# Layer norm's steps among other units, low parts and small parameters behind the sums that units wait for, splits for the keys ahead of those for the queries

## The chip, the core and the metric

One core of a Trainium2 chip runs the kernel. The metric is the time of one execution on the device, in microseconds (us); shorter is better. Five engines work side by side, each in the order of its own program, and are held together by semaphores: TensorE (PE in the profile, PEld for its weight loads), VectorE (DVE), ScalarE (ACT), GpSimd (POOL) and SyncE (SP), which here starts the transfers.

## The reference, cut to what matters

A block of 512 tokens by 1024 features passes through four layers in float32. The parts that the change touches:

```
# even mixer (first layer)
u  = causal_conv(a_val * sigmoid(a_glu), 31 taps)
ya = silu(layernorm(u, ln_g, ln_b)) * silu(a_gate)     # mean, then variance of u - mean
yb = pool branch * silu(b_gate)
h  = h + concat(ya, yb) @ w_out
# odd mixer (second layer): starts with rmsnorm(h, norm_odd) @ w_in
# third layer, at its end
gate = sigmoid(rmsnorm(h, norm_ple) @ w_ple_gate)      # 8 units "gate0"
h    = h + gate * (p @ w_ple_proj)
hk   = rmsnorm(h, kv_norm);   k = rope(hk @ w_k);  v = hk @ w_v
hn   = rmsnorm(h, norm_mix);  q = rope(hn @ w_q)       # fourth layer, attention
```

The third layer's mixer (a state space model) needs some small parameters (powers of a complex number per state) that depend on the inputs alone.

## The kernel before, in words

Everything is held transposed: features on the 128 partitions, the 512 tokens along the free dimension, so `h` is 8 chunks `H[:, c, :]` of 128x512. The weights come in 281 **units** of 128x1024 (8 blocks of 128x128), in the order of the list `ORDER`. A product in float32 precision is made of three faster ones: each operand x is split into a high part (rounded to fp32r) and a low part (what is left), and hi*hi + hi*lo + lo*hi is summed in one PSUM bank. A unit is thus 24 matmuls of 128x512 on TensorE.

For weight unit i, `high` (line 276, ScalarE) makes `WH` once SyncE has fetched `RAW` and unit i-3 is done (3 buffers); `low` (line 280, GpSimd) makes `WL`; SyncE fetches into `RAW` again behind it. The loops of ScalarE and GpSimd call `highs(n + 4)` and `lows(n + 4)` in step n, so the work for unit n+3 is queued there, and everything written behind it in that step waits for unit n. `linear` (line 291) issues one unit: 16 matmuls first, then the 8 with the low weights; with `ready` it waits, chunk by chunk, for the high parts of the input (`x_hi`, ScalarE, line 413), then for the low ones (`x_lo`, VectorE, line 417 or 421), and it wants `WL` from its start.

**Even mixer.** `EVEN` lists the steps: K0 to K7 are the 8 units of `yb @ w_out`, O0 to O7 those of `ya @ w_out`. The convolution's taps (VectorE, line 587) are spread over the steps up to K1. GpSimd adds the 8 chunks into `LS` (`conv_sums`, line 724); TensorE makes the mean behind K2 (line 487); VectorE subtracts it (line 663), ScalarE squares (line 348), GpSimd and VectorE add the squares (lines 357, 363); TensorE sums them over the partitions behind K4 (`stat_sums`, line 375); VectorE adds eps (line 381), GpSimd takes the root (line 386), TensorE spreads it over the partitions inside K5 (`stat_spread`, line 394). In step K6 VectorE and ScalarE then work on each chunk in turn: times the root (line 674), silu (ScalarE, line 563), times the gate (line 682), high and low part of `ya`. O0 waits for these chunks. In steps O0 to O7 VectorE adds each unit's result to `H` (`add_to_h`, line 428), ScalarE makes the high part and a square of it, VectorE the low part for the odd mixer (line 421) and ten of the small parameters' instructions (`dve_params`, lines 1113 to 1184, 128x32 each, in a chain). X0 is the odd mixer's first unit.

**Gates of the third layer.** `pe_ple` runs the 8 units gate0. Per chunk c: VectorE scales the unit's result (`scaled`, line 410), ScalarE takes the sigmoid (line 1950), VectorE multiplies by `PJ` (line 1966) and adds to `H` (line 1969), ScalarE makes two high parts (for keys `P2h`, for queries `P0h`) and a square, VectorE two low parts, GpSimd adds the square. ScalarE does the sigmoid of chunk n and the three operations of chunk n-2 in step n, behind `highs`. The units wk (keys) wait for `P2h` and `P2l` chunk by chunk.

Of the kernel before, what the change touches and what calls it, by code (L numbers as in the profile page):

```python
# [71 lines left out]
TAPS = 6  # L72
PX_AT = {1: 0, 2: 1, 4: 2, 5: 3}
# [66 lines left out]
def program(nc, ctx, known, D):  # L140
# [150 lines left out]
    def linear(pe, what, xh, xl, chunks, freed_by, ready=None, half=None, first=False):  # L291
# [14 lines left out]
        for n, c in enumerate(chunks):  # L306
# [12 lines left out]
            if half and n == 5:  # L319
                half()  # L320
# [129 lines left out]
    def pe_even(pe):  # L450
# [4 lines left out]
        for n, (kind, c) in enumerate(EVEN):  # L455
            what = even_what(n)
            if kind in "GABFS":
                linear(pe, what, P0h, P0l, range(8), "evac_d", "even" if n == 0 else None,
                       {2: lambda: stat_sums(pe, "even", True), 3: lambda: spread_even(pe)}.get(n), n == 0)
# [23 lines left out]
            if (kind, c) == ("K", 2):  # L483
                b, before = banks.take("mean", "ln_sub")
                pe.wait_ge(*at(*before))
                pe.wait_ge(*at("conv_sum", 7))
                pe.matmul(b[:, :], MEAN[:, :], LS[:, :], start=True, stop=True).then_inc(*inc("ln_mean", 0))
            elif (kind, c) == ("K", 4):
                stat_sums(pe, "ln", True)
# [6 lines left out]
    def act_even(act):  # L496
# [37 lines left out]
    def act_even_follow(act, n, s):  # L534
# [18 lines left out]
        elif kind == "K" and s == 0 and c == 2:  # L553
            for i in range(8):
                act.wait_ge(*at("ln_sub", i if i < 7 else "mean"))
                square(act, "ln", i, chunk(i), True)
        elif kind == "K" and s == 0 and c == 6:
            for i in range(9):
                if i < 8:
                    act.wait_ge(*at("ln_n", i if i < 7 else ("spread", "ln")))  # L560
                    if i > 1:
                        act.wait_ge(*at("x_lo", ("ya", i - 2)))
                    act.activation(CB[i % 2][:, :], chunk(i), ACT.Silu, bias=vec("ln_a_b", i),
                                   scale=vec("ln_a_g", i)).then_inc(*inc("ln_silu", i))
                if i > 0:
                    act.wait_ge(*at("ln_y", i - 1))
                    split_hi(act, "ya", i - 1, E2h[:, i - 1, :], CB[(i - 1) % 2][:, :])
                if i == 4:
                    highs(act, IDX[what] + 5)
        elif kind == "O" and s == 0:  # L570
            norm_in_act(act, "odd", c, [("odd", P0h, vec("norm_odd", c))], what)
            if c < 4:
                act_params(act, c)
# [49 lines left out]
    def dve_even_follow(dve, n, s, parameters):  # L623
# [34 lines left out]
        elif kind == "K" and s == 0:  # L658
            if c == 3:
# [8 lines left out]
            elif c == 5:  # L668
                stat_mean(dve, "ln", 1e-5)
            elif c == 6:  # L670
# [30 lines left out]
    def pool_even(pool):  # L701
# [8 lines left out]
        for n in range(len(EVEN) + 3):  # L710
            for s in (3, 2, 1, 0):
                if s == 0 and n < len(EVEN):
                    lows(pool, n + 4)
# [13 lines left out]
    def pool_even_follow(pool, n, s):  # L727
# [32 lines left out]
        elif kind == "K" and s == 0 and c == 2:  # L760
            conv_sums(pool, 3)
            for i in range(8):
                add_square(pool, "ln", i, True)
            stat_root(pool, "ln")
# [1165 lines left out]
    def ple_outs(l, n):  # L1930
        if l:
            return []
        return [("kv", P2h, vec("kv_norm", n)), ("att", P0h, vec("norm_mix", 8 + n))]

    def act_ple(act, l):
        for n in range(9):
            if n < 8:
                highs(act, IDX[(f"gate{l}", 0, n)] + 4)
                if n == 1:
                    stat_copy(act, f"ple{l}")  # L1940
                    act_ple_gate(act, l, 0)
                if n > 0:
                    act_ple_gate(act, l, n)
            if n > 1:
                norm_in_act(act, "out" if l else "att", n - 2, ple_outs(l, n - 2), ("ple", l, n - 2), l == 1)
        norm_in_act(act, "out" if l else "att", 7, ple_outs(l, 7), ("ple", l, 7), l == 1)
# [5 lines left out]
    def dve_ple(dve, l):  # L1952
        for n in range(10):
            if n == 0:
                stat_mean(dve, f"ple{l}")
                continue
            if n == 1:
                scaled(dve, tmp(2), (f"gate{l}", 0, 0), f"ple{l}").then_inc(*inc("evac_d", (f"gate{l}", 0, 0)))
            if n < 8:
                scaled(dve, tmp(2 + n % 4), (f"gate{l}", 0, n), f"ple{l}").then_inc(*inc("evac_d", (f"gate{l}", 0, n)))  # L1960
            if n < 9:
                c = n - 1
                s = tmp(2 + c % 4)
                dve.wait_ge(*at("ple_sig", (l, c)))
                dve.wait_ge(*at("evac_a", ("pj", l, c)))
                dve.tensor_tensor(s, s, PJ[:, c, :], ALU.mult).then_inc(*inc("ple_y", (l, c)))
                dve.wait_ge(*at("ple_y", (l, c)))
                dve.wait_ge(*at("h", (f"down{l}", 3, c)))
# [599 lines left out]
```

## Time and profile before

| | us |
|---|---|
| median of 3 runs | 1908.15 |
| lowest and highest of them | 1906.16, 1908.15 |
| the profiled execution | 1902.84 |
| its span in the trace | 1901.02 |
| TensorE busy | 1776.7 (93% of the span) |
| GpSimd, VectorE, ScalarE busy | 976.5, 894.8, 760.5 |

The profile page and the trace are of one execution. In a timeline a row gives the start and the duration of one or several like instructions, and in square brackets how long the engine had been idle before it and what released it. Matmuls overlap in a timeline: their pace is the distance of their starts. The granted clock is TensorE's, as a share of 2.4 GHz; its two levels are 2.4 and 1.2 GHz.

### The profile page before, as it was taken

Reading aid. Unit: us, or ns where it says so; the run is one execution under the profiler, and the core shown is the slowest. Engines: PE = TensorE matmul, PEld = TensorE weight load, DVE = VectorE, ACT = ScalarE, POOL = GpSimd, SP = SyncE. Lnnn points to the kernel's source line nnn. Section 1 sums busy time; section 2 is a strip of 40 time slices with the busy share of each in tenths; the row PEclk is TensorE's granted clock in tenths of the full one; section 3 lists DMA queues with packets and bytes.
Section 4 is the critical chain, followed back from the end, with each engine's and each line's share of the span. In section 5 each row is a group of like instructions: output and inputs, shape, how many; then the busy total and the mean of one; then the engine's idle time right before and its main releaser. Section 6 shows DMA issues by size and latency. Waiting matters only on the chain.

```text
span 1901.0 us, 20872 instructions
## 1 busy us (share of the span) xinstructions
PE 1776.7 (93%) x7994; PEld 1440.6 (76%) x7994; DVE 894.8 (47%) x1297; ACT 760.5 (40%) x1194; POOL 976.5 (51%) x613
## 2 busy tenths in 40 slices
PE   9999988999998889999999999897888999999996
PEld 7887876777777777888888888674456888888885
DVE  3999956676665874622121213723452221212125
ACT  5233324377765553343232323422454432323242
POOL 5869544577555564644444445652234544444462
PEclk9999999999998899999999999897889999999998
DMA  4323213222221233222232222220001222232221
GB/s 160 109 78 111 100 67 102 87 79 89 89 80 48 80 104 106 94 100 93 95 100 100 90 98 97 70 87 25 23 22 46 99 96 93 100 100 93 96 100 45
DMA packets 55107, 164.04 MB, mean 86 GB/s; under 512 B 6368, under 2 KB 14176, under 8 KB 54880
## 3 DMA queue, kind: packets, MB, share of 16 engines
q1 hardware_dynamic: 55008, 162.71, 25.4%
q8 instruction: 64, 1.05, 0.2%
q14 instruction: 35, 0.29, 0.0%
HBM read 156.66 MB, written 6.03 MB: 86 GB/s over the span
## 4 chain that ended last, share of the span: by engine, by line
PE 67%; DVE 11%; issue 8%; ACT 7%; POOL 7%; DMA 0%; SPq 0%; POOLq 0%; DVEq 0%; ACTq 0%
PE B L304 57%; DVE B L587 3%; POOL WL L280 3%; PE B L287 1%; ACT WH L276 1%; PE B L289 1%; PE B L288 1%; PE B L1616 1%; PE B L2162 1%; PE B L1509 1%; PE B L2144 1%; DVE P0l L421 1%; DVE SW L1113 1%; POOL TMP L2127 1%; ACT TMP L2112 1%
## 5 line engine op out<-in xcount | busy, mean ns | idle before, releaser
L280 POOL TENSOR_TENSOR WL<-RAW,WH 128x1024 fp32r<-128x1024 f32 x281 | 682.8, 2432 | 712.7 <-ACT WH L276 712.7
L276 ACT ACTIVATE WH<-RAW 128x1024 fp32r<-128x1024 f32 x281 | 296.8, 1059 | 743.6 <-PE B L304 713.0
L304 PE MATMUL B<-P0h,WH 128*128 128x512 f32 x1128 | 444.1, 394 | 5.9 <-ACT P0h L413 3.9
L304 PE MATMUL B<-P0l,WH 128*128 128x512 f32 x1128 | 437.0, 393 | 1.0 <-DVE P0l L421 1.0
L304 PE MATMUL B<-P0h,WL 128*128 128x512 f32 x1128 | 284.9, 390 | 2.3 <-POOL WL L280 2.3
L304 PEld LDWEIGHTS B<-P0h,WH 128*128 128x128 f32 x1128 | 213.0, 189 | 55.5 <-issue 5.6
L304 PEld LDWEIGHTS B<-P0l,WH 128*128 128x128 f32 x1128 | 213.8, 190 | 46.3 <-DVE P0l L421 1.5
L304 PEld LDWEIGHTS B<-P0h,WL 128*128 128x128 f32 x1128 | 211.9, 188 | 46.6 <-POOL WL L280 2.7
L428 DVE TENSOR_TENSOR H<-H,B 128x512 f32<-128x512 f32 x96 | 65.8, 686 | 318.9 <-PE B L304 318.9
L304 PE MATMUL B<-P1h,WH 128*128 128x512 f32 x512 | 199.7, 390 | 1.4 <-DVE P1l L417 1.4
L304 PE MATMUL B<-P1l,WH 128*128 128x512 f32 x512 | 194.7, 389 | 0.0
L1882 DVE SCALAR_TENSOR_TENSOR TMP<-B,RS 128x512 f32<-128x512 f32 x64 | 44.1, 691 | 258.4 <-PE B L304 244.0
L587 DVE SCALAR_TENSOR_TENSOR B<-UP,VE,B 128x512 f32<-128x512 f32 x232 | 156.5, 750 | 1.6 <-ACT B L531 1.6
L304 PE MATMUL B<-P1h,WL 128*128 128x512 f32 x512 | 131.0, 389 | 0.0
L304 PEld LDWEIGHTS B<-P1h,WH 128*128 128x128 f32 x512 | 96.1, 188 | 22.1 <-DVE P1l L417 2.3
L304 PEld LDWEIGHTS B<-P1h,WL 128*128 128x128 f32 x512 | 96.1, 188 | 19.9
L304 PEld LDWEIGHTS B<-P1l,WH 128*128 128x128 f32 x512 | 96.1, 188 | 19.9
L357 POOL TENSOR_TENSOR ACC<-ACC,TMP 128x512 f32<-128x512 f32 x51 | 74.1, 1453 | 52.7 <-ACT TMP L348 52.5
L304 PE MATMUL B<-P2h,WH 128*128 128x512 f32 x144 | 56.7, 394 | 9.0 <-ACT P2h L413 9.0
L304 PE MATMUL B<-P2l,WH 128*128 128x512 f32 x144 | 54.3, 402 | 0.0
L421 DVE SCALAR_TENSOR_TENSOR P0l<-H,VE,P0h 128x512 fp32r<-128x512 f32 x40 | 46.0, 1161 | 13.6 <-ACT P0h L413 13.6
L2127 POOL TENSOR_SCALAR TMP<-TMP,AS 128x256 f32<-128x256 f32 (+1 forms) x64 | 27.9, 456 | 44.6 <-DVE AS L2121 44.6
(327 smaller groups left out, 2676.5 us busy)
## 6 DMA issues: line engine op xcount, KB each, us to landing
RAW<-in_w SPq DMA_DIRECT2D x281, 512.0 KB, 3.2
H<-in_xT SPq DMA_DIRECT2D x8, 256.0 KB, 4.6
g<-GB SPq DMA_DIRECT2D x8, 256.0 KB, 2.1
GB<-g SPq DMA_DIRECT2D x32, 64.0 KB, 2.0
out<-TMP SPq DMA_DIRECT2D x8, 256.0 KB, 2.1
u<-TMP SPq DMA_DIRECT2D x7, 256.0 KB, 2.0
U<-u SPq DMA_DIRECT2D x28, 64.0 KB, 2.0
SPT<-in_ssm SPq DMA_DIRECT2D x1, 1040.0 KB, 5.7
```

What stands on the lines that cost most here:

```text
L276: act.activation(WH[:, i % NS, :], RAW[:, i % NR, :], ACT.Copy).then_inc(*inc("w_hi", i))
L280: pool.tensor_tensor(WL[:, i % NS, :], RAW[:, i % NR, :], WH[:, i % NS, :].bitcast(F32), ALU.subtract).then_inc(*inc("w_lo", i))
L287: pe.matmul(out, wh, xh, start=start, stop=False)
L288: pe.matmul(out, wl, xh, start=False, stop=False)
L289: return pe.matmul(out, wh, xl, start=False, stop=stop)
L304: return pe.matmul(b[:, :], w[:, ws[c]], x[:, c, :], start=start, stop=stop)
L357: pool.tensor_tensor(ACC[:, :], ACC[:, :], tmp(c % 2), ALU.add).then_inc(*inc("acc", (k, c)))
L421: dve.scalar_tensor_tensor(dst, src, g, hi.bitcast(F32), ALU.mult, ALU.subtract).then_inc(*inc("x_lo", (k, c)))
L428: dve.tensor_tensor(H[:, n, :], H[:, n, :], banks.bank[what][:, :], ALU.add).then_inc(*inc("h", key))
L587: dve.scalar_tensor_tensor(chunk(c) if j == 30 else CB[c % 2][:, :], UP[:, c, j:j + T], w, CB[c % 2][:, :], ALU.mult, ALU.add).then_inc(*i ...
L1882: dve.scalar_tensor_tensor(mlp_tmp(q, c), banks.bank[what][:, :], 0.0, rs(f"mlp{l}"), ALU.max, ALU.mult).then_inc(*inc("evac_d", what))
L2127: pool.tensor_scalar(s_head(n, h), s_head(n, h), st[:, 16 + h:17 + h], 1.0, ALU.mult, ALU.mult).then_inc(*inc("att_w", (n, h)))
```

## The change

The same instructions are issued, with other places in the engines' orders.

1. **Layer norm.** GpSimd sums the last two conv chunks in step K1, ahead of `low` for that step (it was K2, behind it). The mean's matmul stands inside unit K2, behind its fifth chunk. ScalarE's squares and GpSimd's sums of squares and root come in step K2 ahead of `highs` and `lows`. VectorE subtracts in step K2 (it was K3). The sums over the partitions and the spread are inside K4 (behind chunks 1 and 7), and VectorE and ScalarE do the chain for `ya` in step K4 (it was K6), with the high weights of three units in between.
2. **Small parameters.** 12 of their instructions behind `add_to_h` in each of steps O0 to O4 (it was 10 behind the low part in each of O1 to O6); ScalarE's first function of them moves to K7.
3. **Gates and queries.** ScalarE works on chunk n, and not n-2, behind the sigmoid of chunk n. VectorE makes the low part for the keys of chunk c-1 behind the scaling of chunk c, and the low parts for the queries later: three during the gates, five in `dve_att`. GpSimd adds chunk n's square in step n (it was n+1). The gates of the last layer stay as they are, in functions of their own.

```diff
             elif kind == "K":
                 linear(pe, what, E1h, E1l, range(8), "h", "yb" if c == 0 else None,
-                       (lambda: stat_spread(pe, "ln")) if c == 5 else None)
+                       {2: {4: lambda: ln_mean(pe)},
+                        4: {1: lambda: stat_sums(pe, "ln", True), 7: lambda: stat_spread(pe, "ln")}}.get(c, {}))
...
# ScalarE, in step n
                 if s == 0 and n < len(EVEN):
+                    if EVEN[n] == ("K", 2):
+                        act_ln_squares(act)
+                    elif EVEN[n] == ("K", 4):
+                        act_ln(act, n)
                     highs(act, n + 4)
...
+            if i in (1, 3, 6):
+                highs(act, n + 4 + (1, 3, 6).index(i))
...
# VectorE
         elif kind == "K" and s == 0:
-            if c == 3:
+            if c == 2:
                 dve.wait_ge(*at("ln_mean", 0))
...
-            elif c == 5:
+            elif c == 4:
                 stat_mean(dve, "ln", 1e-5)
-            elif c == 6:
                 dve.wait_ge(*at("stat_spread", "ln"))
...
         elif kind == "O" and s == 0:
             add_to_h(dve, what, c, what, what_k(c))
+            if c < 5:
+                for _ in range(PARAMETERS):
+                    next(parameters, None)
         elif kind == "O" and s == 1:
             split_lo_scaled(dve, "odd", c, P0l[:, c, :], H[:, c, :], vec("norm_odd", c), P0h[:, c, :])
-            if c < 6:
-                for _ in range(10):
-                    next(parameters, None)
...
# GpSimd, in step n
                 if s == 0 and n < len(EVEN):
+                    if EVEN[n] == ("K", 1):
+                        conv_sums(pool, 3)
+                    elif EVEN[n] == ("K", 2):
+                        for i in range(8):
+                            add_square(pool, "ln", i, True)
+                        stat_root(pool, "ln")
                     lows(pool, n + 4)
...
+    def act_ple(act):
+        for n in range(8):
+            highs(act, IDX[("gate0", 0, n)] + 4)
+            if n == 1:
+                stat_copy(act, "ple0")
+            for c in ([0, 1] if n == 1 else [n] if n else []):
+                act_ple_gate(act, 0, c)
+                norm_in_act(act, "att", c, ple_outs(c), ("ple", 0, c))
...
+    def dve_ple(dve):
+
+        stat_mean(dve, "ple0")
+        for c in range(8):
+            scaled(dve, tmp(2 + c % 4), ("gate0", 0, c), "ple0").then_inc(*inc("evac_d", ("gate0", 0, c)))
+            if c > 0:
+                dve_kv(dve, c - 1)
+            dve_ple_sum(dve, 0, c)
+            if c in (2, 3, 4):
+                dve_q_in(dve, [c - 2])
+        dve_kv(dve, 7)
...
     def pool_ple(pool, l):
...
-            if n > 0:
-                add_square(pool, "out" if l else "att", n - 1, l == 1)
+            if l == 0 and n < 8:
+                add_square(pool, "att", n)
+            elif l and n > 0:
+                add_square(pool, "out", n - 1, True)
...
     def dve_att(dve):
+        dve_q_in(dve, (3, 4))
         stat_mean(dve, "att")
+        dve_q_in(dve, (5, 6))
         dve.wait_ge(*at("stat_root", "att"))
         dve.tensor_copy(RK[:, :], SM[:, 8:12]).then_inc(*inc("v_root", 0))
+        dve_q_in(dve, [7])
         dve_rope_in(dve, ("k", 0))
```

## Rows read from the trace of the kernel before

**Rows 1.** Windows, from K2's end to O0's: stretch, length, busy time by engine, granted clock, DMA share, GB/s.
```profile
258.00:317.00 59.00, 45.45 (x187) 34.70 (x186) 26.80 (x43) 21.23 (x30) 23.81 (x13) 0.88 0.24 81
```
**Rows 2.** Timeline of TensorE, K2 to the start of O1: start, duration, what.
```profile
260.20 1.98 PE L304 MATMUL B<-E1h,WL 128*128 128x512 f32 x8
268.34 2.04 PE L487 MATMUL B<-LS,MEAN 128*128 128x512 f32 x2 [6.17 <-POOL LS L724]
...
316.75 0.39 PE L304 MATMUL B<-E2h,WH 128*128 128x512 f32 x1
```
**Rows 3.** Timeline of TensorE around X0: its start, its wait, what follows it.
```profile
354.83 0.39 PE L304 MATMUL B<-P0h,WH 128*128 128x512 f32 x1
...
360.73 0.79 PE L304 MATMUL B<-P0h,WH 128*128 128x512 f32 x1 [3.02 <-ACT P0h L413]
...
367.19 0.95 PE L375 MATMUL B<-MEAN,ACC 128*128 128x1 f32 x8
```
**Rows 4.** Timeline of TensorE: last gate, wait in wk0, what follows it.
```profile
1207.42 1.98 PE L304 MATMUL B<-P1h,WL 128*128 128x512 f32 x8
...
1222.11 0.80 PE L304 MATMUL B<-P2h,WH 128*128 128x512 f32 x1 [6.08 <-ACT P2h L413]
...
1226.55 1.26 PE L375 MATMUL B<-MEAN,ACC 128*128 128x1 f32 x8
```
**Rows 5.** Timeline of GpSimd: the low part of a weight, then the last two conv sums.
```profile
263.40 2.34 POOL L280 TENSOR_TENSOR WL<-RAW,WH 128x1024 fp32r<-128x1024 f32 x1 [3.04 <-ACT WH L276]
265.70 2.49 POOL L724 TENSOR_TENSOR LS<-LS,UP 128x512 f32<-128x512 f32 x2
```
**Rows 6.** Timeline of VectorE: last taps, subtraction of the mean, last sum of squares.
```profile
254.57 1.40 DVE L587 SCALAR_TENSOR_TENSOR UP<-UP,VE,B 128x512 f32<-128x512 f32 x2
...
270.42 3.68 DVE L663 TENSOR_TENSOR UP<-UP,B 128x512 f32<-128x512 f32 x6 [7.52 <-PE B L487]
...
277.75 1.35 DVE L363 TENSOR_TENSOR TMP<-TMP 128x512 f32<-128x512 f32 x1 [0.76 <-ACT TMP L348]
```
**Rows 7.** Chain in order of time: the sums over the partitions, the spread.
```profile
281.83 1.68 PE B L375 x16
...
286.40 0.44 PE B L394 x4
```
**Rows 8.** Timeline of ScalarE: first two silus, last high part of ya.
```profile
296.10 1.47 ACT L563 ACTIVATE B<-UP,VE 128x512 f32<-128x512 f32 x2
...
312.41 0.60 ACT L413 ACTIVATE E2h<-B 128x512 fp32r<-128x512 f32 x1 [0.25 <-DVE B L682]
```
**Rows 9.** Timeline of VectorE in steps O2 and O7: three parameters, the last addition to H.
```profile
328.86 2.83 DVE L1121 SCALAR_TENSOR_TENSOR SW<-SW 128x32 f32<-128x32 f32 x3
...
361.38 0.68 DVE L428 TENSOR_TENSOR H<-H,B 128x512 f32<-128x512 f32 x1
```
**Rows 10.** Timeline of GpSimd in the gates: a square added, then a low part.
```profile
1191.15 1.38 POOL L357 TENSOR_TENSOR ACC<-ACC,TMP 128x512 f32<-128x512 f32 x1 [5.31 <-ACT TMP L348]
1192.49 2.40 POOL L280 TENSOR_TENSOR WL<-RAW,WH 128x1024 fp32r<-128x1024 f32 x1
```
**Rows 11.** Timeline of VectorE in the gates: product with PJ, addition to H, product again.
```profile
1179.42 1.05 DVE L1966 TENSOR_TENSOR TMP<-TMP,PJ 128x512 f32<-128x512 f32 x1
1180.51 0.69 DVE L1969 TENSOR_TENSOR H<-H,TMP 128x512 f32<-128x512 f32 x1
...
1193.72 1.72 DVE L1966 TENSOR_TENSOR TMP<-TMP,PJ 128x512 f32<-128x512 f32 x1
```
**Rows 12.** Timeline of ScalarE in the gates: first sigmoids; then weight, high part, square.
```profile
1178.75 1.23 ACT L1950 ACTIVATE TMP<-TMP 128x512 f32<-128x512 f32 x2 [0.83 <-DVE TMP L410]
...
1187.74 1.06 ACT L276 ACTIVATE WH<-RAW 128x1024 fp32r<-128x1024 f32 x1 [2.10 <-PE B L304]
...
1189.23 0.71 ACT L413 ACTIVATE P2h<-H,VE 128x512 fp32r<-128x512 f32 x1
...
1190.45 0.62 ACT L348 ACTIVATE TMP<-H 128x512 f32<-128x512 f32 x1
```

More of the change, by code:

```diff
@@ L72 @@
 TAPS = 6
+PARAMETERS = 12
 PX_AT = {1: 0, 2: 1, 4: 2, 5: 3}
@@ L289, in mm3, with linear @@
         return pe.matmul(out, wh, xl, start=False, stop=stop)
-    def linear(pe, what, xh, xl, chunks, freed_by, ready=None, half=None, first=False):
+    def linear(pe, what, xh, xl, chunks, freed_by, ready=None, between={}, first=False):
         i = IDX[what]
@@ L318, in linear @@
                 product(wh, xl, c)
-            if half and n == 5:
-                half()
+            if n in between:
+                between[n]()
         if first:
@@ L552, in act_even_follow, with act_ln_squares, act_ln @@
             act.activation(AG[:, c, :], AG[:, c, :], ACT.Silu).then_inc(*inc("ag", c))
[L553 to L569, printed above, removed]
+        elif kind == "K" and s == 0 and c == 7:
+            act_params(act, 0)
         elif kind == "O" and s == 0:
             norm_in_act(act, "odd", c, [("odd", P0h, vec("norm_odd", c))], what)
-            if c < 4:
-                act_params(act, c)
+            if c < 3:
+                act_params(act, c + 1)
+    def act_ln_squares(act):
+        for i in range(8):
+            act.wait_ge(*at("ln_sub", i if i < 7 else "mean"))
+            square(act, "ln", i, chunk(i), True)
+    def act_ln(act, n):
+        for i in range(9):
+            if i < 8:
+                act.wait_ge(*at("ln_n", i if i < 7 else ("spread", "ln")))
+                if i > 1:
+                    act.wait_ge(*at("x_lo", ("ya", i - 2)))
+                act.activation(CB[i % 2][:, :], chunk(i), ACT.Silu, bias=vec("ln_a_b", i),
+                               scale=vec("ln_a_g", i)).then_inc(*inc("ln_silu", i))
+            if i > 0:
+                act.wait_ge(*at("ln_y", i - 1))
+                split_hi(act, "ya", i - 1, E2h[:, i - 1, :], CB[(i - 1) % 2][:, :])
+            if i in (1, 3, 6):
+                highs(act, n + 4 + (1, 3, 6).index(i))
     def norm_in_act(act, k, c, outs, h_key, fast=False):
@@ L759, in pool_even_follow @@
                                ALU.subtract).then_inc(*inc("d_lo", c))
[L760 to L764, printed above, removed]
         elif kind == "O" and s == 0:
@@ L1950, in act_ple_gate @@
         act.activation(tmp(2 + n % 4), tmp(2 + n % 4), ACT.Sigmoid).then_inc(*inc("ple_sig", (l, n)))
[L1952 to L1960, printed above, removed]
-            if n < 9:
[L1962 to L1968, printed above, removed]
-                dve.tensor_tensor(H[:, c, :], H[:, c, :], s, ALU.add).then_inc(*inc("h", ("ple", l, c)))
-            if n > 1:
-                c = n - 2
-                if l == 0:
-                    split_lo_scaled(dve, "kv", c, P2l[:, c, :], H[:, c, :], vec("kv_norm", c), P2h[:, c, :])
-                    split_lo_scaled(dve, "att", c, P0l[:, c, :], H[:, c, :], vec("norm_mix", 8 + c), P0h[:, c, :])
-                elif c % 2 and c > 1:
-                    add_square2(dve, "out", c)
@@ new lines, in dve_q_in @@
+    def dve_q_in(dve, chunks):
+        for c in chunks:
+            split_lo_scaled(dve, "att", c, P0l[:, c, :], H[:, c, :], vec("norm_mix", 8 + c), P0h[:, c, :])
+    def dve_ple(dve):
[8 more added lines that the diff above has]
+        dve_kv(dve, 7)
@@ L1978, in pool_ple, with dve_last_ple @@
+    def dve_last_ple(dve):
+        stat_mean(dve, "ple1")
+        for n in range(1, 10):
+            for c in ([0, 1] if n == 1 else [n] if n < 8 else []):
+                scaled(dve, tmp(2 + c % 4), ("gate1", 0, c), "ple1").then_inc(*inc("evac_d", ("gate1", 0, c)))
+            if n < 9:
+                dve_ple_sum(dve, 1, n - 1)
+            if n > 3 and n % 2:
+                add_square2(dve, "out", n - 2)
     def pool_ple(pool, l):
```

51 lines of the change are left out of this document (29 added, 22 removed).

## The prediction, made before the changed kernel was run

> **What bounds the kernel now.** I first asked for the busy time, the granted clock and the waits of TensorE stretch by stretch. It is busy 93% of the span (the table above), and in the long runs of units it stands still nowhere; what a change of order can win is therefore only its stalls and what the clock loses behind them. The window from K2's end to O0's shows such a place: of 59.00 us TensorE is busy 45.45, at a granted clock of 0.88 [rows 1]. A unit has 24 matmuls and takes (354.83 - 316.75) / 7 = 5.44 us when nothing holds it, O1 to O7 being such a run [rows 2, 3]; one matmul takes 0.227. By that measure I read TensorE's timeline at the three places that the change touches.
>
> - Layer norm: K2 ends at 260.20 + 8 x 0.227 = 262.01, and O1 starts at 316.75 [rows 2]. Between them lie six units, the mean, the sums and the spread. The mean is held 6.17 us by GpSimd's conv sum, and runs at the lower level of the clock, 1.2 GHz (2.04 us for a pair of records) [rows 2].
> - X0: from 354.83 to the sums at 367.19 it takes 12.36 us and not 5.44, the longest wait being 3.02 for a high part of the input [rows 3]. Loss 6.9.
> - wk0: the last gate ends at 1207.42 + 1.81 = 1209.23, wk0 ends at 1226.55 or a little later (I use 1226.7), so 17.5 us and not 5.44; its last wait is 6.08, for the keys' last high part [rows 4]. Loss 12.0.
>
> **Part 1, layer norm: -19.1 us.** Every step gets an earlier place; I follow it through. GpSimd's two sums took 2.49 us and stood behind a low part of 2.34 that itself waited for K2's end [rows 5]. Ahead of it they wait for the taps alone, which end at 254.57 + 1.40 = 255.97 [rows 6]: the last sum ends at about 257.9. K2 starts at 262.01 - 5.44 = 256.57, its tenth matmul ends at 258.84, so the mean finds its input there with 0.9 us to spare. It costs 0.86 to 1.02 (half of 2.04 [rows 2]; I take 0.86, nearest to the matmuls' pace of four times 0.227), so K2 ends at 262.87, K3 at 268.31. From the first subtraction to the end of the last sum of squares it took 277.75 + 1.35 - 270.42 = 8.7 us [rows 6], now from 259.8 to 268.5. K4 wants it behind its fourth matmul, at 269.2: 0.7 to spare. The sums take 1.68 [rows 7], to 270.9; the root lies between the end of the sums at 283.51 and the spread at 286.40, which did not wait for it [rows 7], so it takes under 2.89; now the spread stands 12 matmuls on, at 273.6, 2.72 later, which leaves a wait of 0.2 at most. The spread takes 0.44 [rows 7]. The weights of K5, whose `high` is now behind the squares (done by about 268.5) and whose `low` is behind the root (done by 273.6 + 2.4 = 276.0), are wanted at 275.85 and, the low ones, at 279.5: nothing waits. SyncE fetches O0's weight behind K5's low part, and ScalarE wants it at 281.7, over 5 us later. The chain for `ya` took 312.41 + 0.60 - 296.10 = 16.9 us [rows 8] and did not start until K6 was done, because of the `highs` ahead of it. It now starts at 274.8 and ends at 291.7; the three `high` in it fit where ScalarE waited for VectorE. TensorE is through K7 at 262.87 + 5 x 5.44 + 1.68 + 0.44 = 292.2, so O0 finds all eight chunks and ends at 297.6 and not 316.75: 19.1 us, both stalls and the slow stretches behind them. Nothing is late next; the margins are the cover of this part, and past them TensorE waits inside a unit.
>
> **Part 2, the parameters: -4.5 us.** VectorE, not TensorE, sets X0's start of chunks 6 and 7: its last addition to H begins at 361.38, 6.5 us behind O7's end [rows 3, 9]. The parameters are short by themselves, but three of them could take 2.83 us [rows 9], held by GpSimd (part 3 has the rows for that). The number of instructions stays 48, in 60 places. What changes is that the addition to H goes ahead of them, that they fill the 0.8 us in which VectorE waited for ScalarE's high part (0.71, the row is given in part 3, and the semaphores; five times, 4.0 us), that they start one step sooner, and that O5 to O7 have none. From O0's end at 316.75 [rows 2] to 361.38 + 0.68 = 362.06 [rows 9] VectorE had 45.3 us of this work; less 4.0 it is 41.3, so from 297.6 the last addition ends at about 339 at best and, laid out instruction by instruction against GpSimd's weights, at 341.5. Chunk 7 is wanted 3.2 us into X0, which would start at 335.7, so at 338.9, and has its high part 0.7 behind the addition. The loss is then 0.8 to 3.3 of the 6.9; I take 2.4. Bounds: 0 and -6.9.
>
> **Part 3, keys ahead of queries: +5 us.** This part I expect to cost. On VectorE it takes work off the path; but it makes ScalarE wait, inside step c, for VectorE's product and addition for the same chunk, and the weight for unit c+3, the next sigmoid and all its high parts queue behind that wait. The product reads two SBUF operands. Where GpSimd is at work on two SBUF operands it ends some 0.55 behind GpSimd: started at 1193.72 in a low part of 1192.49 to 1194.89, it ended at 1195.44 [rows 10, 11]; free of it such an instruction takes 0.69 [rows 11]. Step c, from its weight's start T: sigmoid ends at T + 1.49 + 0.1 (1187.74 to 1189.23 [rows 12]), product ready at T + 1.64. GpSimd in that time: its square's sum starts at T + 0.18 and takes 1.3, and the low part of the weight follows at once [rows 10], at T + 1.43 to T + 3.84. So the product arrives 0.2 us behind it and ends at T + 4.39; the addition at T + 5.12; ScalarE's three operations take 1.22 + 0.52 = 1.74 [rows 12]; next step at T + 6.9. That is above TensorE's 5.44, so ScalarE never catches up. Chunks 0 and 1: first sigmoid 1178.75 to 1179.4, product to 1180.47, addition to 1181.2 [rows 11, 12], then 1.74, a sigmoid, a product and an addition without GpSimd, and 1.74: step 2 starts at 1186.8. Step 7 starts at 1186.8 + 5 x 6.9 = 1221.3, its key part begins 5.15 later and takes 0.71 [rows 12]: 1227.2, where it was there at 1222.1 [rows 4]. The remaining ten matmuls are at the lower clock in either kernel. Difference +5.1. The weights of the gates still come in time (the last at T_4 + 1.06 = 1201.7, wanted at 1203.8). The low parts for the queries in `dve_att` lie under wk1 (three of 0.7, or up to 2.4 more behind one low part [rows 10], in 5.44 us) and cost nothing; were that cover gone, 2 us.
>
> The Trainium skill ("SBUF — State Buffer", section "Who interferes with whom") says that a VectorE instruction with two SBUF inputs and a GpSimd instruction that reads SBUF exclude each other for the whole instruction, and that the one issued later waits. The row of 1.72 us agrees. By that rule what decides is who issues first, which is why 0.2 us weighs so much here.
>
> **The rivals.** (a) ScalarE keeps up: the product is issued ahead of the low part, say because the sum of the square is held a little. A step is then 1.64 + 0.69 + 0.73 + 1.74 = 4.8 us, under 5.44; chunk 7 is ready at about 1213.1, and wk0 loses next to nothing: -11.4 in place of +5, in all -35, 1873. For it: the race is of 0.2 us. Against it: every product in the trace that met a low part waited. (b) The margins of part 1 (0.9, 0.7, 1.3) don't hold, for instance because GpSimd is slower on the squares; TensorE then waits inside K4 and falls to the lower clock, and half of part 1 is lost: -9, 1899. (c) The change does not do what it says: the stalls come back where the work was moved to, O0 and X0 wait as before: 1908. (d) Slower: the loop of part 3. If the addition, too, is held by a GpSimd instruction, a step grows by 2.4 and more; the weights of the gates come late as well. The gain of 23.6 from parts 1 and 2 is eaten when chunk 7 comes 23.6 after 1222.1, which needs (1245.7 - 1186.8 - 5.9) / 5 = 10.6 us a step in place of 6.9. At 11.5 a step it is +4.5: 1913. Against it: behind the low part GpSimd waits for that step's square, so nothing of it can hold the addition.
>
> **How the numbers follow.** -19.1 - 4.5 + 5.0 = -18.6. The profiled execution took 1902.84 (span 1901.02 and 1.8 around it), so the like of it would take 1884.2; it lay 5.3 under the median, so I predict 1908.15 - 18.6 = 1889.5. The forecast has 0.62, with its own range from 1882 to 1900 (part 1 at 12 to 19, part 2 at 0 to 7, part 3 at 0 to 8). (a) has 0.13, (b) 0.12, (c) 0.06, (d) 0.07. The range takes in (a) and (b) and leaves out (c), (d): 1872 to 1900. A measurement of this kernel tells some 0.2%, 3.8 us, from no change. Faster by more: 0.62 + 0.13 + 0.12 = 0.87; within it 0.06; slower 0.07.
>
> **What would show it.** Part 1: TensorE has no wait at line 487 and O1 starts near 297.6; a wait of TensorE at line 375 or 394 inside K4 would be (b). Part 2: X0 takes 6 to 9 us and its wait is for `P0h`. Part 3: ScalarE's weights in the gates start 6.9 us apart, products at line 1966 take some 2.8 us, wk0 first waits some 2 us for its low weights and then twice some 6 us for `P2h`, and takes 22.6 us from the last gate's end to its own, not 17.5. Steps of 5.44 there would be (a). The prediction is wrong, too, if the stretches outside these three places change by more than 2 us.

## The result, and the profile after

| | before | after |
|---|---|---|
| median, us | 1907.20 (4 runs, 1906.16 to 1908.15) | 1883.66 (4 runs, 1882.80 to 1884.30) |
| profiled execution, its span | 1902.84, 1901.02 | 1884.06, 1882.2 |

The ratio is 0.9878 (95%: 0.9863 to 0.9893): 23.5 us faster, where 18.6 was forecast; 1883.66 lies 5.8 under the predicted 1889.5 and inside the range. Between the two profiled executions the span fell by 18.8.

TensorE's timelines give the stretches below, as the distances of their first matmuls (before from [rows 2 to 4] and the same places of its timeline).

| stretch, us | before | after | difference |
|---|---|---|---|
| K2's start to the mean | 11.77 | 2.27 | -9.50 |
| the mean to O1 | 48.41 | 39.04 | -9.37 |
| O1 to X0 | 38.08 | 38.08 | 0.00 |
| X0 to its sums | 12.36 | 6.96 | -5.40 |
| these sums to the last gate's end | 842.04 | 843.25 | +1.21 |
| the last gate's end to the sums behind wk0 | 17.32 | 22.20 | +4.88 |
| these sums to wo, the attention's last product | 214.29 | 214.21 | -0.08 |
| from there to the end | 460.16 | 460.11 | -0.05 |

K2 itself starts 0.5 earlier (256.08 for 256.57); with it the differences add up to -18.8.

The windows of after, K2's end to O1 and the gates' last part with wk0 (columns as in [rows 1]):

```profile
258.00:298.00 40.00, 40.00 (x186) 33.02 (x185) 27.05 (x43) 23.06 (x33) 21.10 (x11) 1.00 0.26 89
1190.00:1215.00 25.00, 15.20 (x57) 11.69 (x55) 16.24 (x15) 8.78 (x14) 12.89 (x7) 0.70 0.21 69
```

Where TensorE was busy 45.45 of 59 us at a clock of 0.88 [rows 1], it is now busy throughout, at 1.00. The other place is worse than it was.

**Layer norm.** TensorE's timeline of after, the rows that answer to [rows 2, 7]:

```profile
258.35 1.02 PE L490 MATMUL B<-LS,MEAN 128*128 128x512 f32 x2
...
268.77 0.28 PE L376 MATMUL B<-MEAN,ACC 128*128 128x1 f32 x2
...
270.25 0.36 PE L376 MATMUL B<-MEAN,TMP 128*128 128x1 f32 x2
...
273.33 0.60 PE L395 MATMUL B<-CO,SM 128*128 128x128 f32 x4
...
297.39 0.39 PE L305 MATMUL B<-E2h,WH 128*128 128x512 f32 x1
```

The 6.17 us in front of the mean are gone, no row from here to O1 has a wait, and the mean's pair runs at full clock (1.02, it was 2.04). The same stretch on GpSimd, which answers to [rows 5]:

```profile
254.90 2.53 POOL L739 TENSOR_TENSOR LS<-LS,UP 128x512 f32<-128x512 f32 x2 [0.45 <-DVE UP L597]
...
270.89 1.02 POOL L387 TENSOR_TENSOR SM<-SM 128x4 f32<-128x4 f32 x1 [3.37 <-DVE SM L382]
```

And on VectorE, beside [rows 6]:

```profile
259.40 3.68 DVE L673 TENSOR_TENSOR UP<-UP,B 128x512 f32<-128x512 f32 x6 [2.44 <-PE B L490]
...
266.73 1.34 DVE L364 TENSOR_TENSOR TMP<-TMP 128x512 f32<-128x512 f32 x1 [0.76 <-ACT TMP L349]
```

The sums end at 257.43 and the mean wants them at 258.35; the squares end at 268.07 and TensorE wants them at 268.77; the root is there at 271.91 and the spread stands at 273.33. ScalarE's timeline, beside [rows 8]: the chain for `ya` runs from 274.69 to 291.62, inside K5 to K7.

```profile
274.69 1.49 ACT L577 ACTIVATE B<-UP,VE 128x512 f32<-128x512 f32 x2 [5.51 <-DVE UP L683]
...
291.02 0.60 ACT L414 ACTIVATE E2h<-B 128x512 fp32r<-128x512 f32 x1 [0.25 <-DVE B L691]
```

**X0.** TensorE's timeline of after (beside [rows 3]):

```profile
335.47 0.39 PE L305 MATMUL B<-P0h,WH 128*128 128x512 f32 x1
...
341.21 0.50 PE L305 MATMUL B<-P0l,WH 128*128 128x512 f32 x1 [0.36 <-DVE P0l L422]
342.43 1.02 PE L376 MATMUL B<-MEAN,ACC 128*128 128x1 f32 x8 [0.71 <-POOL ACC L358]
```

VectorE's, beside [rows 9]:

```profile
337.02 0.68 DVE L429 TENSOR_TENSOR H<-H,B 128x512 f32<-128x512 f32 x1
338.49 2.67 DVE L422 SCALAR_TENSOR_TENSOR P0l<-H,VE,P0h 128x512 fp32r<-128x512 f32 x1 [0.79 <-ACT P0h L414]
```

GpSimd's at the same time:

```profile
338.22 2.39 POOL L281 TENSOR_TENSOR WL<-RAW,WH 128x1024 fp32r<-128x1024 f32 x1
```

VectorE's last addition to `H` comes 1.6 us into X0, not 6.5; TensorE waits for no high part. What is left, 1.5 us, is the last low part, which took 2.67 because it was issued 0.3 behind GpSimd's low part and ended 0.55 behind its end, and the square's sum behind it.

**Gates.** VectorE's timeline in one step (beside [rows 11]):

```profile
1178.67 2.77 DVE L1973 TENSOR_TENSOR TMP<-TMP,PJ 128x512 f32<-128x512 f32 x1 [1.47 <-ACT TMP L1967]
1181.48 0.69 DVE L1976 TENSOR_TENSOR H<-H,TMP 128x512 f32<-128x512 f32 x1
```

GpSimd's, beside [rows 10]:

```profile
1177.25 1.29 POOL L358 TENSOR_TENSOR ACC<-ACC,TMP 128x512 f32<-128x512 f32 x1 [3.25 <-ACT TMP L349]
1178.51 2.39 POOL L281 TENSOR_TENSOR WL<-RAW,WH 128x1024 fp32r<-128x1024 f32 x1
```

ScalarE's, beside [rows 12]:

```profile
1177.08 1.05 ACT L277 ACTIVATE WH<-RAW 128x1024 fp32r<-128x1024 f32 x1
...
1182.20 0.72 ACT L414 ACTIVATE P2h<-H,VE 128x512 fp32r<-128x512 f32 x1 [3.56 <-DVE H L1976]
...
1183.97 1.04 ACT L277 ACTIVATE WH<-RAW 128x1024 fp32r<-128x1024 f32 x1
```

GpSimd's low part starts 0.16 us ahead of the product, which ends 0.54 behind it. ScalarE stands 3.56 us, and its steps are 1183.97 - 1177.08 = 6.89 apart, over a unit's 5.44. TensorE stands 2.00 us at wk0's first matmul (1187.84), which starts when GpSimd's low part of its weight is done (1187.75). Then, in wk0 and wk1 (beside [rows 4]):

```profile
1196.64 0.80 PE L305 MATMUL B<-P2h,WH 128*128 128x512 f32 x1 [4.22 <-ACT P2h L414]
...
1203.45 0.80 PE L305 MATMUL B<-P2h,WH 128*128 128x512 f32 x1 [5.58 <-ACT P2h L414]
...
1207.88 1.27 PE L376 MATMUL B<-MEAN,ACC 128*128 128x1 f32 x8
...
1209.57 0.39 PE L305 MATMUL B<-P2h,WH 128*128 128x512 f32 x1
1209.80 0.40 PE L305 MATMUL B<-P2l,WH 128*128 128x512 f32 x1
```

### The profile page after: what moved, and what is told of

It is laid out like the page before. It is cut to its first block, busy times and chain, and to the rows that moved or that the text cites. A ratio compares the mean times of both kernels' runs of the same rounds, so it can differ in the third digit from the quotient of the medians.

```text
span 1882.2 us, 20872 instructions
## 1 busy us (share of the span) xinstructions
PE 1772.0 (94%) x7994; PEld 1439.0 (76%) x7994; DVE 892.6 (47%) x1297; ACT 759.9 (40%) x1194; POOL 973.0 (52%) x613
## 4 chain that ended last, share of the span: by engine, by line
PE 59%; ACT 7%; DVE 6%; issue 6%; POOL 4%; DMA 0%; POOLq 0%; SPq 0%; DVEq 0%; ACTq 0%
PE B L305 50%; POOL WL L281 2%; ACT WH L277 1%; PE B L288 1%; PE B L290 1%; PE B L289 1%; PE B L2193 1%; DVE TMP L1973 1%; PE B L1626 1%; PE B L2175 1%; PE B L1519 1%; DVE SW L1123 1%; POOL TMP L2158 1%; ACT TMP L2143 1%; POOL RP L2055 1%
## 5 line engine op out<-in xcount | busy, mean ns | idle before, releaser
L305 PE MATMUL B<-R2h,WH 128*128 128x512 f32 x128 | 49.8, 389 | 0.0
```

Source lines behind the costliest of these rows:

```text
L305: return pe.matmul(b[:, :], w[:, ws[c]], x[:, c, :], start=start, stop=stop)
```

## The experiments

All times are medians of four runs (e2: eleven, e4: six) with their ratio to the kernel before on the same chip (its median there was 1905.90 to 1907.20). The last two columns are stretches of the trace: the last gate's end to the sums behind wk0, and these sums to wo. A trace is of one execution, and that can lie off the median of its kernel: e7's took 1878.11 (6.1 under), e2's 1910.75 (3.5 over), e8's 1892.71 (2.9 over), the others' at most 1.5 from it.

| kernel | us | ratio (95%) | gates to sums | sums to wo |
|---|---|---|---|---|
| after | 1883.66 | 0.9878 (0.9863 to 0.9893) | 22.20 | 214.21 |
| e1, parts 1 and 2 | 1881.64 | 0.9872 (0.9858 to 0.9885) | 17.31 | 217.70 |
| e2, part 3 | 1907.21 | 1.0007 (0.9999 to 1.0016) | 21.85 | 213.19 |
| e3, part 1 | 1887.68 | 0.9902 (0.9887 to 0.9917) | 17.31 | 217.67 |
| e4, part 2 | 1900.48 | 0.9968 (0.9956 to 0.9979) | 16.73 | 214.49 |
| e5, gate in PSUM | 1868.32 | 0.9800 (0.9786 to 0.9815) | 8.29 | 213.65 |
| e6, ScalarE one chunk behind | 1880.53 | 0.9864 (0.9849 to 0.9879) | 18.42 | 212.93 |
| e7, sigmoid first | 1884.23 | 0.9876 (0.9858 to 0.9895) | 19.96 | 212.91 |
| e8, conv sums behind the low part | 1889.86 | 0.9907 (0.9890 to 0.9923) | 22.23 | 214.26 |
| e9, after once more | 1884.17 | 0.9887 (0.9872 to 0.9902) | 22.10 | 213.50 |
| e10, e1 once more | 1882.58 | 0.9874 (0.9854 to 0.9895) | 17.32 | 217.48 |
| e11, gate in PSUM, part 3 undone | 1876.50 | 0.9848 (0.9833 to 0.9863) | 11.92 | 215.92 |
| e12, e5 with two weights later | 1872.93 | 0.9831 (0.9812 to 0.9849) | 9.96 | 215.22 |

### The parts alone

**e1, parts 1 and 2.** After, with the gates' functions and `dve_att` of before; and the same once more beside after (e10, e9).

```diff
-        act_ple(act)
+        act_ple(act, 0)
-        dve_ple(dve)
+        dve_ple(dve, 0)
```

> The changed kernel with part 3 (gates, keys ahead of queries) undone. Theory A (the three parts add up, part 3 costs): K2's start to O1's start takes 41.3 us and X0 to its sums 7.0 as in the changed kernel, the last gate's end to the sums behind wk0 17.3 as in the kernel before; 4.9 us faster than the changed kernel, about 1878.8 in the timed runs, 24.3 us (1.3%) under the kernel before in the trace. Rival B (part 3 costs only in the profiled execution, where the kernel before was 4.4 us under its own median): within 1 us of the changed kernel in the timed runs, about 1883.7.

> The changed kernel as it is, beside the next one on the same chip, to set the price of part 3 in timed runs against that in the trace. Theory A (4.9 us, of which the stretch behind it gives part back by spending less time at the lower clock): the last gate's end to the sums 22.2 us, from these sums to wo 213 to 215 us, in all 2 to 3 us slower than parts 1 and 2 alone. Rival B (the full 4.9 in the timed runs, the earlier difference of 2 was scatter): 4 to 6 us slower than the next one.

> Parts 1 and 2 without part 3, beside the changed kernel. Theory A: last gate's end to sums 17.3 us, from the sums to wo 216 to 218 us (3 more than with part 3), about 2 to 3 us faster than the changed kernel. Rival B: from the sums to wo as long as with part 3, 4 to 6 us faster.

TensorE's timeline of e1, wk0 and wk1:

```profile
1197.47 0.80 PE L305 MATMUL B<-P2h,WH 128*128 128x512 f32 x1 [6.08 <-ACT P2h L414]
...
1201.90 1.70 PE L376 MATMUL B<-MEAN,ACC 128*128 128x1 f32 x8
...
1204.46 0.63 PE L305 MATMUL B<-P2h,WH 128*128 128x512 f32 x1
1204.89 0.63 PE L305 MATMUL B<-P2l,WH 128*128 128x512 f32 x1
```

At its place part 3 costs 22.20 - 17.31 = 4.9 us (4.8 in e9 against e10), as forecast. But e1 then takes 3.5 us longer from the sums to wo (4.0 in e10 against e9), with the same work and waits. Half of it is to be seen here: in wk1 e1's matmuls are 0.43 apart, the lower level of the clock, and after's, in the rows of wk1 above, are 0.23 apart; e1's next mark, the spread behind wk1, stands 8.44 behind the sums and after's 6.69.

The windows show both halves (columns as in [rows 1]). First the 4.5 us behind the sums, in before, after and e1:

```profile
1226.55:1231.05 4.50, 4.50 (x24) 3.94 (x23) 0.16 (x1) 1.06 (x1) 3.07 (x2) 0.93 0.00 0
1207.88:1212.38 4.50, 4.50 (x24) 3.92 (x23) 3.19 (x3) 1.06 (x1) 3.07 (x2) 0.93 0.00 0
1201.90:1206.40 4.50, 4.50 (x16) 3.91 (x15) 0.16 (x1) 1.06 (x1) 3.06 (x2) 0.51 0.00 0
```

Then 65.6 to 69.2 us behind the sums, in after and e1:

```profile
1273.48:1277.08 3.60, 3.60 (x17) 2.74 (x15) 0.00 (x0) 0.00 (x0) 0.00 (x0) 1.00 0.00 0
1267.50:1271.10 3.60, 3.60 (x10) 2.83 (x9) 0.00 (x0) 0.00 (x0) 0.00 (x0) 0.50 0.00 0
```

So the other half is the clock too. The next stretch at the lower level lies 55.3 to 65.5 us behind the sums in after and 59.1 to 69.3 in e1, where it takes in more matmuls; 86.1 to 89.6 us behind the sums it is 17 of them at 1.00 in after and 8 at 0.50 in e1. By these two places and one 127 us behind the sums the distance grows from 1.75 to 3.5. That the longer wait brings the shorter stretch behind it doesn't follow: before has e1's waits in wk0 (2.61 and 6.08; 2.62 and 6.08 in e1), and behind the sums it is like after. What set when the low level ended is open.

e1 falls between its two theories. In the times part 3 costs 2.0 us (1883.66 against 1881.64) and 1.6 (1884.17 against 1882.58), and the intervals overlap. So the wait is real, and its price in the end is 0 to 2.

**e2, part 3 alone**: before, with the gates' functions and `dve_att` of after. **e3, part 1 alone**: e1 with the parameters where they were.

```diff
# e2, to before
-        act_ple(act, 0)
-        dve_ple(dve, 0)
+        act_ple(act)
+        dve_ple(dve)
# e3, to e1
             add_to_h(dve, what, c, what, what_k(c))
-            if c < 5:
-                for _ in range(PARAMETERS):
-                    next(parameters, None)
...
             split_lo_scaled(dve, "odd", c, P0l[:, c, :], H[:, c, :], vec("norm_odd", c), P0h[:, c, :])
+            if c < 6:
+                for _ in range(10):
+                    next(parameters, None)
```

> The kernel before with part 3 alone. Theory A: +4.9 us against the kernel before, from the stretch between the last gate's end and the sums behind wk0 (22.2 and not 17.3 us), every step of the gates 6.85 us. Rival B: no difference in the timed runs. Rival C (the loss comes of the order of parts, not of part 3): this stretch stays at 17.3.

> The kernel before with layer norm's steps moved alone. Theory A: -18.9 us, all between K2's start and O1's start (41.3 and not 60.2 us); X0 stays at 12.4 us. Rival: the late parameters take part of it, because O1 to O7 come 19 us earlier while the parameters take as long: X0 longer than 12.4, gain below 17.

e2 is at 1907.21 and before at 1907.19 on the same chip: part 3 by itself moves nothing in the times (interval -0.2 to +3 us), with 4.5 us more at wk0 in its trace. e3 gains 19.5 us, and its X0 still takes 12.45. In e2's trace the stretch from the mean to O1 takes 50.57 and not the 48.41 of before, though nothing of it was changed. Its windows in before and in e2 (columns as in [rows 1]) show the clock at 0.90 and at 0.84:

```profile
268.34:316.75 48.41, 41.02 (x167) 31.33 (x168) 26.06 (x41) 20.18 (x29) 16.80 (x9) 0.90 0.22 77
269.90:320.50 50.60, 43.71 (x167) 33.17 (x168) 26.02 (x41) 20.28 (x29) 16.77 (x9) 0.84 0.21 74
```

**e4, part 2 alone**: before, with 12 instructions behind `add_to_h` in O0 to O4.

```diff
         elif kind == "O" and s == 0:
             add_to_h(dve, what, c, what, what_k(c))
+            if c < 5:
+                for _ in range(12):
+                    next(parameters, None)
```

> The kernel before with the small parameters moved alone. Theory A: -5.4 us, X0 to its sums 7.0 and not 12.4 us. Rival: VectorE is later at O0 here than in the changed kernel, where it was idle 4 us before O0's end, so the gain is only 3 us or less and X0 still waits for P0h.

It gains 6.7 us (4.0 to 8.4 by the interval); behind part 1 the same change gains 6.0 (e3 to e1). X0 takes 6.93 to its sums as in after, so the rival is out. The mean to O1 takes 50.34, as in e2.

### Part 3: what holds the product

**e5, the gate in PSUM.** Scaled result, sigmoid and product stay in the unit's own PSUM bank, so the product and the addition each have one operand in SBUF and not two.

```diff
+    def gate_buf(l, c):
+        return tmp(2 + c % 4) if l else banks.bank["gate0", 0, c][:, :]
...
-            linear(pe, (f"gate{l}", 0, n), *mlp_norm(l), range(8), "evac_d", ...)
+            linear(pe, (f"gate{l}", 0, n), *mlp_norm(l), range(8), "evac_d" if l else ("h", ("ple", 0, n)), ...)
...
-            scaled(dve, tmp(2 + c % 4), ("gate0", 0, c), "ple0")
+            scaled(dve, gate_buf(0, c), ("gate0", 0, c), "ple0")
```

> The changed kernel, but in the gates of the third layer the scaled unit, its sigmoid and the product with PJ stay in the unit's own PSUM bank, so that the product and the addition to H have one operand in SBUF and not two. Same instructions, same order. Theory A (VectorE's product waits for GpSimd's low part because both read two operands from SBUF): products take 0.7 us and not 2.7, a step of ScalarE is 4.8 us of its own and so keeps TensorE's 5.44, the last high part for the keys comes 19 us earlier against the last gate's end, wk0 takes 5.5 to 7 us and not 22.2: -15 to -16.5, about 1868. Rival (the product waits for something else, or the step is long because ScalarE waits in order): products stay above 2 us or steps at 6.8, no gain.

VectorE's timeline of e5:

```profile
1183.21 0.70 DVE L1978 TENSOR_TENSOR B<-B,PJ 128x512 f32<-128x512 f32 x1 [1.81 <-ACT B L1969]
1183.94 0.69 DVE L1981 TENSOR_TENSOR H<-H,B 128x512 f32<-128x512 f32 x1
```

GpSimd's of e5:

```profile
1183.08 2.41 POOL L281 TENSOR_TENSOR WL<-RAW,WH 128x1024 fp32r<-128x1024 f32 x1
```

TensorE's of e5, in wk0:

```profile
1190.21 0.50 PE L305 MATMUL B<-P2h,WH 128*128 128x512 f32 x1 [2.27 <-ACT P2h L414]
```

The product is issued 0.13 us behind GpSimd's low part, as in after, and takes 0.70 and not 2.77. The steps fall from 6.9 to 4.8 to 5.1, TensorE waits once, 2.27 in place of 4.22 and 5.58, and the gates to the sums take 8.29. 1868.32 is 15.3 us under after: this version beats both kernels. The two SBUF operands were the cause. It is the operands that are read that count: the addition, from 1183.94, reads one operand from SBUF and one from PSUM and writes to SBUF, and takes 0.69 under the same low part. The low parts of the inputs still read two, and where one meets GpSimd it is held as before (one of the queries', at 1194.04, takes 2.92).

**e7, sigmoid first.** ScalarE's high part of the weight goes behind the sigmoid, so that the product is issued ahead of GpSimd's low part.

```diff
-            highs(act, IDX[("gate0", 0, n)] + 4)
+            if n < 2:
+                highs(act, IDX[("gate0", 0, n)] + 4)
...
             for c in ([0, 1] if n == 1 else [n] if n else []):
                 act_ple_gate(act, 0, c)
+                highs(act, IDX[("gate0", 0, n)] + 4)
                 norm_in_act(act, "att", c, ple_outs(c), ("ple", 0, c))
```

> The changed kernel, but in the gates' steps ScalarE does the sigmoid ahead of the weight's high part. Theory A: the product is then done ahead of GpSimd's low part, but the addition to H behind it is held by it for the same time: a step goes from 6.85 to about 6.7 us, in all -1 us or less. Rival (the 1 us of the weight's high part ahead of the sigmoid is what makes the step long; no holding): a step of 5.9, wk0 5 us shorter.

VectorE's timeline of e7:

```profile
1174.75 1.37 DVE L1975 TENSOR_TENSOR TMP<-TMP,PJ 128x512 f32<-128x512 f32 x1 [0.52 <-ACT TMP L1969]
1176.15 2.77 DVE L1978 TENSOR_TENSOR H<-H,TMP 128x512 f32<-128x512 f32 x1
```

The product is let go sooner, behind the square's sum, and the addition, which reads two SBUF operands too, is caught by the low part in its stead: 2.77. A step is 6.62 (it was 6.89), as theory A has it, and the time is 1884.23. An order that saves one instruction hands the next one over.

**e6, ScalarE one chunk behind.** The high parts of chunk n-1 behind the sigmoid of chunk n, so that ScalarE does not wait for the product.

```diff
             for c in ([0, 1] if n == 1 else [n] if n else []):
                 act_ple_gate(act, 0, c)
-                norm_in_act(act, "att", c, ple_outs(c), ("ple", 0, c))
+            for c in ([n - 1] if n else []):
+                norm_in_act(act, "att", c, ple_outs(c), ("ple", 0, c))
```

> The changed kernel, but ScalarE does the high parts and the square of chunk n-1 behind the sigmoid of chunk n, and those of chunk 7 at the end; VectorE's order is that of the change. Theory A (the loss is the closed loop ScalarE - VectorE - ScalarE inside one step, longer than 5.44): the loop is open, steps are 5.44, wk0 waits only for the last chunk, some 3 us: wk0 takes 8 to 10 us and not 22.2, -12 to -14, about 1870.5. Rival (VectorE's own work, held by GpSimd, is what lasts, as in the kernel before): wk0 at 15 to 17 us, -5 to -7.

A miss by 10 us against theory A, and nearer to the rival. VectorE's timeline of e6:

```profile
1177.43 0.68 DVE L411 TENSOR_TENSOR TMP<-B,RS 128x512 f32<-128x512 f32 x1
1179.42 0.75 DVE L422 SCALAR_TENSOR_TENSOR P2l<-H,VE,P2h 128x512 fp32r<-128x512 f32 x1 [1.31 <-ACT P2h L414]
1180.09 0.68 DVE L1975 TENSOR_TENSOR TMP<-TMP,PJ 128x512 f32<-128x512 f32 x1
1180.81 1.67 DVE L1978 TENSOR_TENSOR H<-H,TMP 128x512 f32<-128x512 f32 x1
1182.40 2.87 DVE L422 SCALAR_TENSOR_TENSOR P0l<-H,VE,P0h 128x512 fp32r<-128x512 f32 x1
```

The product is free (0.68), but now VectorE's low part for the keys, which stands ahead of it, waits 1.31 for ScalarE's high part, and that stands behind the next sigmoid, which waits for VectorE's scaling, which is behind the held low part of 2.87. The loop is closed through VectorE's order, and such a step is 7.8 us, longer than after's 6.9. There are three of them, those with a low part for the queries; the two behind them, without one, are 4.9 and 5.1. wk0 takes 18.42 and not 22.20, and the time is 3.1 us under after's, with intervals that overlap. Taking a wait away from one engine of a loop does not open it. The hold works the other way round too. GpSimd's timeline of e6, where its low part is issued while VectorE's addition runs and takes 2.83, not 2.39:

```profile
1181.89 2.83 POOL L281 TENSOR_TENSOR WL<-RAW,WH 128x1024 fp32r<-128x1024 f32 x1
```

**e11, the gate in PSUM with part 3 undone** (the same edit as e5's, made to e1), and **e12, e5 with two weights later**: no high part of a weight in step 7, and in step 1 behind the first sigmoid.

```diff
# e11, to e1
-            scaled(dve, tmp(2 + n % 4), (f"gate{l}", 0, n), f"ple{l}")
+            scaled(dve, gate_buf(l, n), (f"gate{l}", 0, n), f"ple{l}")
# e12, to e5
         for n in range(8):
-            highs(act, IDX[("gate0", 0, n)] + 4)
+            if n not in (1, 7):
+                highs(act, IDX[("gate0", 0, n)] + 4)
...
                 act_ple_gate(act, 0, c)
+                if n == 1:
+                    highs(act, IDX[("gate0", 0, n)] + 4)
```

> Parts 1 and 2, the gates in the order of before, but with the gates' product kept in PSUM as in the run before (product and addition with one SBUF operand). Theory A (the held instructions are the cause, the order counts for little once they are gone): product and addition take 0.7 us each; VectorE has 2.1 us for them and two low parts that can still be held, under 5.44 + 1 a step; ScalarE is two chunks behind, so at the end it still has chunks 6 and 7 to do: wk0 9 to 12 us, about 1871. Rival (the new order is what lets the PSUM version win): wk0 15 to 17 us as before, about 1880.

> The changed kernel with the gates' product in PSUM, and ScalarE's weight in step 1 behind the first sigmoid and not ahead of the copy of the root, that of step 7 behind its high parts. Theory A (what is left of wk0's wait, 2.3 us, is ScalarE's delay of 1.8 us in step 7 and the weight ahead of the last sigmoid): both weights off the path, wk0 6 to 7 us and not 8.3, -1.5 to -2.3, about 1866.4. Rival (VectorE's low parts set the last step): wk0 stays at 8.3, no gain.

e11 gains 6.1 us over e10 by PSUM alone (the intervals just overlap), and e5 is 8.2 under e11 (ratios 0.9848 and 0.9800, intervals apart). So e11's theory A, that the order counts for little, missed by 5.5 us, and its rival by 3.5: part 3's order, worth nothing or less in after, is worth several us once the product isn't held. In the two traces 3.6 us of it lie at wk0 and 2.3 in the stretch behind; 1.7 stand already at K2's start, where the two kernels don't differ. e12 missed: it is 4.6 us slower than e5 (the intervals just overlap) where 1.5 to 2.3 faster was expected. TensorE's timeline of e12:

```profile
1188.65 0.50 PE L305 MATMUL B<-P2h,WH 128*128 128x512 f32 x1 [0.78 <-ACT P2h L414]
...
1194.49 1.02 PE L376 MATMUL B<-MEAN,ACC 128*128 128x1 f32 x8 [3.25 <-POOL ACC L358]
```

GpSimd's of e12:

```profile
1190.77 2.35 POOL L281 TENSOR_TENSOR WL<-RAW,WH 128x1024 fp32r<-128x1024 f32 x1 [3.49 <-ACT WH L277]
1193.08 1.26 POOL L358 TENSOR_TENSOR ACC<-ACC,TMP 128x512 f32<-128x512 f32 x1
```

The wait for the keys fell to 0.78 as meant. But GpSimd's order still has the low part for the weight ahead of the last square's sum; the later high part holds both, and TensorE waits 3.25 us for the sum instead. wk0 takes 9.96 and not 8.29, and the stretch behind it is 1.6 longer as well. I had moved a step on ScalarE and not looked past it on GpSimd's queue.

### Part 1: the margin of the mean

**e8**: the conv sums stay in K1, but behind that step's low part.

```diff
-                    if EVEN[n] == ("K", 1):
-                        conv_sums(pool, 3)
                     lows(pool, n + 4)
+                    if EVEN[n] == ("K", 1):
+                        conv_sums(pool, 3)
```

> The changed kernel, but GpSimd's last two conv sums stand behind the low part of step K1, not ahead of it. Theory A (the mean inside K2 has under 1 us to spare): the sums end at about 262.4 and not 257.5, TensorE waits 4 us at the mean, drops to the lower clock for some matmuls, and all that hangs on the mean comes later by as much: +4 to +6. Rival (the chain for ya has slack later): the wait shows at the mean, but the layer norm's later waits shrink and less than 2 us is left.

TensorE's timeline of e8, the mean:

```profile
263.78 1.10 PE L490 MATMUL B<-LS,MEAN 128*128 128x512 f32 x2 [3.93 <-POOL LS L739]
```

The mean is held 3.93 us; the time is 1889.86, 6.2 over after. From K2's start to the mean it takes 6.36 and not 2.27, from the mean to O1 40.71 and not 39.04, so the edit costs 4.09 + 1.67 = 5.8 in the trace. (O1 is 7.1 later; the other 1.34 are there at K2's start, 257.42 and not 256.08.) So the place ahead of the low part is a third of part 1's gain, and the 1.67 behind the wait is matmuls at the lower clock: in the 4 us from the mean on it is at 0.65.

## Why the prediction was right, and where it was not

- **Part 1, -19.1.** From K2's start to O1 the profiled executions differ by 18.9, the runs by 19.5 (e3). Every place held: mean with 0.9 us to spare (0.9 forecast), sums with 0.7 (0.7), chain for `ya` 274.7 to 291.6 (274.8 to 291.7), O1 at 297.39 (297.6). Only the spread has 1.4 to spare where a wait of up to 0.2 was allowed for: the root takes 1.02 us, and 2.89 was its bound. Rivals (b) and (c) are out.
- **Part 2, -4.5.** It is 5.4 in the trace, 6.7 (4.0 to 8.4) in the runs alone and 6.0 behind part 1. The mis-sized step is the last addition to `H`: laid out for 341.5, at best for 339, it began at 337.02 and ended at 337.7. So X0 does not wait for `P0h`, though I had said it would, but for the last low part, held to 2.67, and the square's sum: 1.5 us, where 2.4 was left to pay.
- **Part 3, +5.** The mechanism is right in each step: the product issued 0.16 behind GpSimd's low part (0.2 forecast), 2.77 long (2.8), steps of 6.89 (6.9), wk0 22.20 long (22.6). e5 shows the cause by taking one operand away. The Trainium skill's rule ("SBUF — State Buffer", section "Who interferes with whom": a VectorE instruction with two SBUF inputs and a GpSimd instruction that reads SBUF exclude each other for a whole instruction) agrees with it: 2.77 with two, 0.70 with one. The held product ends 0.54 behind the low part, a little less than the 0.69 that it takes when free. What failed is the step from the wait to the end of the kernel: +5 at its place, but 0 to 2 us in the times. I took the rest of the kernel to stay as it was. So it did between the traces of before and after (no stretch outside the three places by more than 1.2 us), but beside e1 and e10 the stretch from the sums to wo is 3.5 to 4.0 us shorter with part 3, all of it by the clock. Rivals (a) and (d) are out. (a) was also priced wrongly: I had let the product through and forgotten the addition behind it, which reads two SBUF operands as well; in e7 the product is early, the addition is held 2.77, and a step is 6.62 and not 4.8.
- **The sum.** -18.6 in the span, -18.8 measured. That is partly luck: part 3's place and the stretch ahead of it came 1.1 above the forecast, part 2 0.9 under it, and K2 started 0.5 earlier, for which nothing had been forecast. In the times the terms are part 1 -19.5, part 2 -6.0, part 3 +2.0 (e3, e1 and after in turn), together -23.5: by them 3.0 of the miss is part 3's price and 1.5 part 2's gain, neither clear of the intervals. Another 0.9 is the median of before, 1907.20 over four runs and 1908.15 over the three that I had.
- **From the span to the median.** Here is the miss of 5.8. I put the 5.3 us by which the profiled execution of before lay under its median onto both kernels. Of after's runs the profiled one (1884.06) is 0.4 over the median, so without the offset the forecast is 1884.2. Where the 5.3 us sit is shown only in part. e2 and e4 have the layer norm of before, and in their traces O1 comes 3.7 and 3.3 us later. Of this 2.2 and 1.9 lie between the mean and O1 (50.57 and 50.34, not 48.41), in the stretch that part 1 makes 39.04 in each of its traces but e8's: that much goes away with the change. But 1.6 and 1.3 stand already at K2's start (258.14 and 257.90, not 256.57), and e6 and e11, which have part 1, start K2 at 257.8 too. A third place is the sums to wo, 214.3 in before's trace and 217.5 to 217.7 in e1, e3 and e10 with the same order of the gates; by it e3's trace is only 15.6 shorter than before's, where its time is 19.5 shorter. Before's other executions have no trace, so what makes up its 5.3 is open. Nor does part 1 free a kernel of such an offset: e7's profiled execution lies 6.1 under its median.

## What to carry to other kernels

- An offset between one profiled execution and the median isn't a constant (5.3 us in before, 0.4 the other way in after, 6.1 in e7): don't carry it from one kernel to another, but ask which stretch it sits in, and whether the change removes that stretch. Waits of TensorE are the first suspects, since here the time at the lower clock behind one differed between executions of the same steps.
- When an engine is to work closer behind another, look at what is issued beside it for its whole length: here a product issued 0.16 us behind GpSimd's low part took 2.1 us more, in a loop of ScalarE and VectorE that had no room for it. Give the product an operand in PSUM rather than juggle the order: e7 moved the hold from the product to the addition, and e6 to the low part for the queries.
- A step moved on one engine moves what waits for it in the other engines' queues (e12), so follow each product of the moved step to the instruction queued behind its user.

## What the runs showed that I had not expected

- What a wait costs is not settled at its end. After has 4.9 us more at wk0 than e1, and comes out of it at the full clock (matmuls 0.23 apart within 1.7 us of the sums), while e1 is still at 0.43 for 4.3 us; and before, with e1's waits, comes out like after. The difference goes on for 130 us, as stretches at the lower level fall on more or fewer matmuls.
- VectorE's low part, which has two SBUF operands and a scalar, is held like the product: 2.67 at X0 in after, 2.87 in e6, where free ones take 0.75.
- With one operand in PSUM a VectorE instruction ran its full pace under GpSimd's low part, 0.70 us, where the same product from two SBUF buffers took 2.77.
